# A diffusion block on one core: modulation vectors summed as 64 partial rows for each half of the columns

## Chip, cores and metric

The kernel runs on one core of a Trainium2 chip. The metric is the device time of one launch in microseconds; the time before is the median of three runs, 2196.51 us (2195.15 to 2198.44).

## The reference

Two blocks follow each other on a sequence of 256 tokens of width 1024, in fp32. The first has two layers of half an FFN (SwiGLU, 2816 wide), a token mixer with two attentions, and another half FFN. The second has two layers as well: retention and gated linear attention over a latent and a context stream, then windowed attention, each followed by an MLP of width 4096. Before and behind every part the stream is scaled, shifted and gated by modulation vectors of 1024 numbers:

```python
# first block, for each of 2 layers: 9 vectors
mod = jax.nn.silu(c) @ ada_w[l] + ada_b[l]          # ada_w[l]: 1024 x 9216
# second block, for each of 2 layers, once with c and once with c_ctx: 6 vectors
m = jax.nn.silu(cvec) @ w_mod[i] + b_mod[i]         # w_mod[i]: 1024 x 6144
```

So each vector is the product of one row of 1024 numbers with a 1024 x 1024 piece of weights, 4 MB. There are 38 of them that are used; the change touches 36, and the first two (`ada(0,1)` and `ada(0,0)`) are made in another way, which stays.

## The kernel before

All weights come from HBM. The large products run on PE in chunks of 1 MB of weights: 322 chunks, with three buffers. Each chunk is loaded by SP's queue into `stage`, ACT rounds it to the format of PE (`whi`, L1504, two halves of 128x1024), DVE takes the difference (`wlo`, L2027, two halves), and PE multiplies with both parts (L626 to L636, L733 to L735). PE waits for `lo_done` of a chunk; ACT waits for `chunk_used` before it overwrites a buffer. The order of work on every engine is written out by hand, chunk by chunk ("window" w below is what ACT and DVE do while PE works on chunk w of a phase). The phases are F0, in0, gate0, out0, F1, F2, in1, gate1, out1, F3, evc, evoc, evx, evox, Mc, M0, odc, odx, odo, M1; F are FFNs, in/gate/out a mixer, ev the retention part for context (c) and latent (x), M the MLPs, od the windowed attention.

Beside this stream the modulation vectors are made. A vector's weights are viewed as 8 blocks of 128 rows: row `k*128 + p` lies on partition p. POOL's queue loads them in four quarters of 1 MB (two k-blocks of 1024 columns, 4 KB runs) into one of two buffers `modw` (L607), each after both steps on the quarter two before are done. DVE makes eight steps for a vector (`mod_steps`, L2049 the first, a plain product; L2052 the seven others, product and sum), each over 128x1024 with a per-partition scalar `cact[:, which, t]`, the Silu of c, and each after the one before (semaphore `mod_step`). The result is 128 partial rows of 1024 columns. PE then transposes it in eight pieces of 128x128 into two banks of PSUM (`turn_mod`, L838), and DVE sums each transposed piece along its 128 columns (`take_mod`, L2060) into 8 columns of `mcol` and adds the bias (L2062). How many steps DVE makes in which window is a table:

```python
STEPS = {
    "F0": [0] + 22 * [1] + 4 * [2] + [0, 0, 1, 1, 0, 0],
    "in0": [2, 2, 2, 2, 0, 1, 1, 3, 3],
    "gate0": [2, 1, 1, 1, 1, 1, 1],
    "evc": [2, 2, 2, 0, 1, 1, 1, 2, 2, 1, 2, 0],
    "evx": [1, 1, 0, 1, 1, 0, 1, 2, 2, 2, 1, 0],
    "Mc": [0] + 3 * [1, 1, 1, 1, 2] + [1, 2, 0, 2, 2, 0, 1, 1, 0, 2, 2, 0, 1, 2, 0, 0],
    "M1": [0, 0] + 8 * [1] + 22 * [0],
}
```

F1 to F3 are as F0, in1 and gate1 as in0 and gate0, M0 as Mc. A turn stands on PE behind the window in which a vector's last step falls, or, in four cases, between the column sums of a normalisation and the filler products that keep PE busy until it is done (`rms_stat`).

At the start ACT's queue loads a part of the constants, the three vectors c as 24 rows of 128 (`crow`), and x; PE transposes `crow` (L900, its first instruction), ACT takes the Silu (`cact`). POOL meanwhile loads the eight quarters of the first two vectors, SP the biases and other small parameters. PE then sums the first two vectors (L922, L929) with filler products between, and SP's second weight chunks wait for their end (`rows1`).

## Time and profile before

| | |
|---|---|
| median of the runs | 2196.51 us |
| the profiled execution | 2197.7 us, its span 2195.9 us |
| PE busy | 2124.2 us, 97% |
| DVE busy | 1783.9 us, 81% |
| ACT busy | 1175.7 us, 54% |
| POOL busy | 109.5 us, 5% |
| mean share of the DMA engines | 69% |
| granted clock of PE, mean | 0.992 |

The span runs from the first to the last instruction. PE's busy time counts matmuls that overlap in the pipeline, so it says that PE had work, not that it was at its peak. What another engine adds counts only where PE, or whatever is last, waits for it; the chain of waits shows where.

### The profile page before, as it was taken

To read this page: it belongs to the slowest core of one execution; us is meant where nothing else is said; L and a number is where in the kernel's file an instruction comes from. 1 tells how busy PE (TensorE), PEld (TensorE's weight loads), DVE (VectorE), ACT (ScalarE), POOL (GpSimd) and SP (SyncE) were. 2 spreads that over 40 slices of the span, in tenths; PEclk is the share of its full clock that TensorE was granted. 3 is DMA by queue.
4 is the path that set the end of the run, shared out by engine and by line. 5 is a ranking of instruction groups with operands and counts; after the bars stand their busy time and mean duration, and the time that the engine had idled before them with its cause. 6 is when DMAs were issued, how large, how long until landed. Compare 5 with 4: busy or idle time off the path is not lost.

```text
span 2195.9 us, 33377 instructions
## 1 busy us (share of the span) xinstructions
PE 2124.2 (97%) x13779; PEld 1860.3 (85%) x13788; DVE 1783.9 (81%) x2366; ACT 1175.7 (54%) x1756; POOL 109.5 (5%) x157
## 2 busy tenths in 40 slices
PE   7999999999999999999999999999999999999997
PEld 4888888888888889898888889888888888768886
DVE  4888787788878878877888777788998998788764
ACT  3554556455455545665544645447645744485742
POOL 1000000000000000000000000000000000000000
PEclk9999999999999999999999999999999999999999
DMA  9888676488868877655887737638878977404662
GB/s 333 284 275 315 222 234 201 146 268 277 304 202 275 289 263 246 214 174 191 277 287 252 262 119 234 230 111 292 287 269 282 296 258 247 135 17 156 213 211 77
DMA packets 331023, 506.51 MB, mean 231 GB/s; under 512 B 12391, under 2 KB 239942, under 8 KB 330871
## 3 DMA queue, kind: packets, MB, share of 16 engines
q1 hardware_dynamic: 288647, 342.01, 47.4%
q0 software_dynamic: 41616, 160.44, 21.2%
q8 instruction: 109, 1.79, 0.3%
q10 hardware_dynamic: 608, 1.92, 0.3%
q14 instruction: 43, 0.35, 0.0%
HBM read 503.29 MB, written 1.05 MB: 230 GB/s over the span
## 4 chain that ended last, share of the span: by engine, by line
PE 83%; DVE 11%; DMA 3%; ACT 2%; issue 1%; POOL 0%; DVEq 0%; POOLq 0%
PE banks L632 36%; PE banks L636 18%; PE banks L626 6%; PE banks L628 6%; PE banks L627 6%; DVE wlo L2027 2%; DMA plain_xs<-in_ada_w_dram 1%; DVE arena L2052 1%; PE banks L838 1%; PE banks L733 1%; PE banks L900 1%; PE banks L734 1%; PE banks L735 1%; DMA modw<-in_w_mod_dram 1%; DMA stage<-in_ffn_wg_dram 1%
## 5 line engine op out<-in xcount | busy, mean ns | idle before, releaser
L2027 DVE TENSOR_TENSOR wlo<-stage,whi 128x1024 fp32r<-128x1024 f32 x644 | 758.3, 1219 | 133.6 <-ACT whi L1504 132.7
L1504 ACT CAST whi<-stage 128x1024 fp32r<-128x1024 f32 x644 | 643.9, 1051 | 336.2 <-PE banks L636 256.5
L632 PE MATMUL banks<-xs,whi 128*128 128x512 f32 x2176 | 688.2, 398 | 14.2 <-DVE xs L2309 9.6
L636 PEld LDWEIGHTS banks<-xs,wlo 128*128 128x128 f32 x2176 | 409.9, 188 | 97.0
L636 PE MATMUL banks<-xs,wlo 128*128 128x256 f32 x2176 | 428.6, 278 | 0.0
L626 PE MATMUL banks<-xs,whi 128*128 128x256 f32 x1216 | 352.0, 289 | 10.4 <-DVE xs L2309 5.7
L632 PEld LDWEIGHTS banks<-xs,whi 128*128 128x128 f32 x2176 | 332.3, 189 | 19.2 <-DVE xs L2309 7.6
L627 PE MATMUL banks<-xs,whi 128*128 128x256 f32 x1216 | 344.6, 283 | 0.0
L628 PE MATMUL banks<-xs,wlo 128*128 128x256 f32 x1216 | 344.5, 283 | 0.0
L632 PE MATMUL banks<-hidden_arena,whi 128*128 128x512 f32 x992 | 311.9, 396 | 0.2 <-DVE wlo L2027 0.2
L2052 DVE SCALAR_TENSOR_TENSOR arena<-modw,cact,arena 128x1024 f32<-128x1024 f32 x217 | 277.9, 1281 | 10.2 <-DMA modw<-in_w_mod_dram 7.2
L626 PEld LDWEIGHTS banks<-xs,whi 128*128 128x128 f32 x1216 | 233.6, 192 | 20.8 <-issue 9.1
L627 PEld LDWEIGHTS banks<-xs,whi 128*128 128x128 f32 x1216 | 233.8, 192 | 0.9 <-issue 0.5
L628 PEld LDWEIGHTS banks<-xs,wlo 128*128 128x128 f32 x1216 | 233.7, 192 | 0.0
L636 PEld LDWEIGHTS banks<-hidden_arena,wlo 128*128 128x128 f32 x992 | 186.5, 188 | 42.6
L636 PE MATMUL banks<-hidden_arena,wlo 128*128 128x256 f32 x992 | 195.8, 279 | 0.0
L632 PEld LDWEIGHTS banks<-hidden_arena,whi 128*128 128x128 f32 x992 | 150.1, 188 | 0.8 <-DVE wlo L2027 0.4
L607 POOL DMA_DIRECT2D modw<-in_w_mod_dram x80 | 57.1, 714 | 1139.7 <-DVE arena L2052 946.6
L632 PE MATMUL banks<-hs,whi 128*128 128x512 f32 x336 | 105.6, 395 | 0.0
L1524 ACT COPY hid<-banks 128x512 f32<-128x512 f32 x44 | 25.9, 588 | 112.8 <-PE banks L636 112.8
L607 POOL DMA_DIRECT2D modw<-in_ada_w_dram x64 | 45.7, 714 | 754.1 <-DVE arena L2052 669.1
L1520 ACT COPY hid<-banks 128x512 f32<-128x512 f32 x44 | 25.9, 588 | 106.0 <-PE banks L636 106.0
(438 smaller groups left out, 2628.8 us busy)
## 6 DMA issues: line engine op xcount, KB each, us to landing
stage<-in_mlp_w_dram SPq DMA_DIRECT2D x96, 1024.0 KB, 5.3
modw<-in_w_mod_dram POOLq DMA_DIRECT2D x80, 1024.0 KB, 5.8
modw<-in_ada_w_dram POOLq DMA_DIRECT2D x66, 1024.0 KB, 5.5
stage<-in_ffn_wg_dram SPq DMA_DIRECT2D x44, 1024.0 KB, 5.4
stage<-in_ffn_wu_dram SPq DMA_DIRECT2D x44, 1024.0 KB, 7.3
stage<-in_ffn_wd_dram SPq DMA_DIRECT2D x44, 1024.0 KB, 7.3
stage<-in_ev_w_in_dram SPq DMA_DIRECT2D x24, 1024.0 KB, 6.1
stage<-in_w_in_dram SPq DMA_DIRECT2D x18, 1024.0 KB, 6.0
```

The costliest lines, as they stand in the source:

```text
L607: pool.dma_start(modw[:, c % 2, :].rearrange("p (a b) -> p a b", a=2), src).then_inc(mod_landed[c % 2], 16)
L626: mm(out, hi, xh, start=first_mm, stop=False, skip_group_check=True)
L627: mm(out, hi, xl, start=False, stop=False, skip_group_check=True)
L628: return mm(out, lo, xh, start=False, stop=last_mm, skip_group_check=True)
L632: return mm(out, whi[:, s, w:w + P], pair.rearrange("p a t -> p (a t)"), start=first_mm, stop=False, skip_group_check=True)
L636: return mm(out[:, 0:T], wlo[:, s, w:w + P], pair[:, 0, :], start=False, stop=last_mm, skip_group_check=True)
L733: mm(out, xh, hi, start=k == 0, stop=False, skip_group_check=True)
L1504: nc.scalar.copy(halves(whi[:, s, :], n, h, True), halves(stage[:, s, :], n, h)).then_inc(hi_done, 1)
L1520: done(nc.scalar.copy(hid[:, j % 2, :, :], R[:, 0:2, T:2 * T]), ("gate", name, j))
L1524: done(nc.scalar.copy(hid[:, 2, :, :], R[:, 2:4, T:2 * T]), ("up", name, j - 1))
L2027: last = v.tensor_tensor(halves(wlo[:, s, :], n, h, True), halves(stage[:, s, :], n, h), halves(whi[:, s, :], n, h, True).bitcast(F32), AL ...
L2052: v.scalar_tensor_tensor(out=acc, in0=w, scalar=cc, in1=acc, op0=ALU.mult, op1=ALU.add).then_inc(mod_step, 1)
```

## The change

The 1024 rows of a vector's weights are viewed as 16 blocks of 64 rows. The left 512 columns are summed on partitions 0 to 63, the right 512 on partitions 64 to 127: 64 partial rows for each half, side by side on the partitions. A step of DVE is over 128x512, and there are 16 for a vector, two where one was. A quarter is loaded by two transfers of 64 partitions, each of four blocks by 512 columns (2 KB runs), and its semaphore counts 32. The transposes are four for a vector, all in one bank; in each transposed piece the left 64 columns belong to the left half's partial rows, the right 64 to the right half's, and one reduction over 128x512 sums both into the 8 columns. For the scalars, c is also laid out in blocks of 64, twice (`half_crow`, 48 rows of 128): six small transfers more on ACT's queue before x, one transpose more, and the Silu over 72 columns in place of 24. The first two vectors keep the old layout of c.

```diff
-        crow = table[0:24, 0:P]
+        crow, half_crow = table[0:24, 0:P], table[0:48, P:2 * P]
+        cact = cond[:, 0:24].rearrange("p (a k) -> p a k", a=3)
+        half_cact = cond[:, 24:72].rearrange("p (a k) -> p a k", a=3)
...
-        macc_of = lambda m: ACC_ROOMS[acc_name(m)]
+        macc_of = lambda m: ACC_ROOMS[acc_name(m)][:, 0:512]
...
-                for q, src in enumerate(quarters(*mods[m][0:3])):
+                w, l, v = mods[m][0:3]
+                rows = w[l].rearrange("(k p) n -> p k n", p=64)
+                for q in range(4):
                     c = 4 * m + q
                     if c >= 2:
-                        pool.wait_ge(mod_step, 2 * (c - 1))
-                    pool.dma_start(modw[:, c % 2, :].rearrange("p (a b) -> p a b", a=2), src).then_inc(mod_landed[c % 2], 16)
+                        pool.wait_ge(mod_step, 4 * (c - 1))
+                    for h in range(2):
+                        a = v * 1024 + 512 * h
+                        pool.dma_start(modw[64 * h:64 * h + 64, c % 2, :].rearrange("p (a b) -> p a b", a=4), rows[:, 4 * q:4 * q + 4, a:a + 512]) \
+                            .then_inc(mod_landed[c % 2], 16)
...
-                pe.wait_ge(mod_step, 8 * (m + 1))
+                pe.wait_ge(mod_step, 16 * (m + 1))
                 if m > 0:
                     pe.wait_ge(mod_taken, m)
-                for k in range(KB):
-                    last = nc.tensor.transpose(banks[:, k // 4, (k % 4) * P:(k % 4 + 1) * P], macc_of(m)[:, k * P:(k + 1) * P], ident)
+                for k in range(4):
+                    last = nc.tensor.transpose(banks[:, 0, k * P:(k + 1) * P], macc_of(m)[:, k * P:(k + 1) * P], ident)
                 last.then_inc(mod_turned, 1)
...
-            pe.wait_ge(c_landed, 48)
-            transpose(R[:, 2, 0:3 * KB], crow, 24).then_inc(pe_out.sem, pe_out.next("c"))
+            pe.wait_ge(c_landed, 144)
+            transpose(R[:, 2, 0:24], crow, 24)
+            transpose(R[:, 2, 24:72], half_crow, 48).then_inc(pe_out.sem, pe_out.next("c"))
...
+            for a, src in enumerate((A["c"].rearrange("b (k p) -> (b k) p", p=64), A["c_2"].rearrange("b (k p) -> (b k) p", p=64),
+                                     A["c_ctx_2"].rearrange("(k p) -> k p", p=64))):
+                for h in range(2):
+                    act.dma_start(half_crow[16 * a:16 * a + 16, 64 * h:64 * h + 64], src).then_inc(c_landed, 16)
             act.dma_start(xrows,
                           A["x"].rearrange("b (a p) d -> p (b a) d", p=P)).then_inc(x_landed, 16)
...
-                for _ in range(count):
-                    m, t = stepped[0] // 8, stepped[0] % 8
-                    stepped[0] += 1
-                    c = 4 * m + t // 2
-                    if t % 2 == 0:
-                        dve.wait_ge(mod_landed[c % 2], 16 * (c // 2 + 1))
-                    w = modw[:, c % 2, (t % 2) * 1024:(t % 2) * 1024 + 1024]
-                    cc = cact[:, mods[m][3], t:t + 1]
+                for i in range(2 * stepped[0], 2 * (stepped[0] + count)):
+                    m, t = i // 16, i % 16
+                    c = 4 * m + t // 4
+                    if t % 4 == 0:
+                        dve.wait_ge(mod_landed[c % 2], 32 * (c // 2 + 1))
+                    w = modw[:, c % 2, (t % 4) * 512:(t % 4) * 512 + 512]
+                    cc = half_cact[:, mods[m][3], t:t + 1]
...
                     if t == 0:
...
                     else:
-                        dve.wait_ge(mod_step, 8 * m + t)
+                        dve.wait_ge(mod_step, 16 * m + t)
                         v.scalar_tensor_tensor(out=acc, in0=w, scalar=cc, in1=acc, op0=ALU.mult, op1=ALU.add).then_inc(mod_step, 1)
...
-                v.tensor_reduce(cols, banks.rearrange("p a (k n) -> p (a k) n", k=4), AX_X, ALU.add).then_inc(mod_taken, 1)
+                v.tensor_reduce(cols.rearrange("p (h k) -> p h k", h=2), banks[:, 0, :].rearrange("p (k h n) -> p h k n", k=4, h=2), AX_X, ALU.add) \
+                    .then_inc(mod_taken, 1)
```

## Rows read from the trace of the kernel before

**Rows 1.** The page, busy time by engine.

```profile
PE 2124.2 (97%) x13779; PEld 1860.3 (85%) x13788; DVE 1783.9 (81%) x2366; ACT 1175.7 (54%) x1756; POOL 109.5 (5%) x157
```

**Rows 2.** The chain of work that ended last, by line, shares of the span.

```profile
by line: PE banks L632 36.2%; PE banks L636 18.0%; PE banks L626 6.2%; PE banks L628 6.0%; PE banks L627 6.0%; DVE wlo L2027 1.9%; DMA plain_xs<-in_ada_w_dram 1.3%; DVE arena L2052 1.1%; PE banks L838 1.1%; issue 1.1%; PE banks L733 1.0%; P
```

**Rows 3.** Groups by line and shape: count, busy us, mean ns, idle time before.

```profile
L2052 DVE SCALAR_TENSOR_TENSOR arena<-modw,cact,arena 128x1024 f32<-128x1024 f32 x217 | 277.9, 1281 | 10.2 <-DMA modw<-in_w_mod_dram 7.2 <-DVE mcol L2062 0.3 <-DMA modw<-in_ada_w_dram 0.2
...
L607 POOL DMA_DIRECT2D modw<-in_w_mod_dram x80 | 57.1, 714 | 1139.7 <-DVE arena L2052 946.6 <-DVE plain_hs L2052 104.4 <-DVE table L2052 83.1
...
L2060 DVE TENSOR_REDUCE mcol<-banks 128x8 f32<-128x1024 f32 x36 | 43.9, 1220 | 7.6 <-PE banks L838 7.5
...
L2049 DVE TENSOR_SCALAR arena<-modw,cact 128x1024 f32<-128x1024 f32 x31 | 23.3, 752 | 4.2 <-PE banks L838 3.5
...
L2812 DVE TENSOR_SCALAR arena<-arena,ecol 128x512 f32<-128x512 f32 x32 | 14.1, 484 | 0.6
...
L2451 DVE TENSOR_REDUCE ecol<-banks 128x2 f32<-128x512 f32 x16 | 11.0, 688 | 4.7 <-PE banks L982 4.4
...
L2523 DVE SCALAR_TENSOR_TENSOR arena<-arena,ecol 128x512 f32<-128x512 f32 x4 | 2.8, 750 | 0.3
```

**Rows 4.** Timeline of DVE: start, us, instruction.

```profile
1565.12 2.60 DVE L2052 SCALAR_TENSOR_TENSOR arena<-modw,cact,arena 128x1024 f32<-128x1024 f32 x2
1567.64 2.35 DVE L2027 TENSOR_TENSOR wlo<-stage,whi 128x1024 fp32r<-128x1024 f32 x2
...
385.82 0.75 DVE L2523 SCALAR_TENSOR_TENSOR arena<-arena,ecol 128x512 f32<-128x512 f32 x1
386.60 1.35 DVE L2229 TENSOR_TENSOR xs<-arena,xs 128x512 fp32r<-128x512 f32 x2
```

**Rows 5.** The chain in order of time: start, us, what.

```profile
276.22 0.87 PE banks L838 x8
...
295.57 1.21 DVE arena L2052
...
316.15 1.28 DVE plain_hs L2052
...
1240.81 1.28 DVE arena L2052
...
1404.29 5.54 DMA modw<-in_w_mod_dram
...
1591.61 5.53 DMA modw<-in_w_mod_dram
...
1626.40 7.53 DMA modw<-in_w_mod_dram
...
1833.45 1.06 PE banks L838 x8
```

**Rows 6.** Timeline of DVE in M0; in brackets the idle time and its releaser.

```profile
1779.60 1.28 DVE L2052 SCALAR_TENSOR_TENSOR arena<-modw,cact,arena 128x1024 f32<-128x1024 f32 x1 [0.90 <-DMA modw<-in_w_mod_dram]
...
1816.33 1.28 DVE L2052 SCALAR_TENSOR_TENSOR arena<-modw,cact,arena 128x1024 f32<-128x1024 f32 x1 [2.00 <-DMA modw<-in_w_mod_dram]
```

**Rows 7.** Waits: who for whom, us in total, times, longest.

```profile
DVE hid L2149 <- ACT hid L1556: 40.0, 41, 2.3
...
PE banks L1195 <- DVE hid L2654: 5.4, 1, 5.4
```

**Rows 8.** Timeline of the start, ACT queue and PE.

```profile
2.12 0.38 ACTq L1637 DMA_DIRECT2D table<-in_c_ctx_dram  x1
...
8.05 0.27 PE L900 MATMUL banks<-base,table 24*128 24x24 f32 x1 [8.05 <-DMA table<-in_c_ctx_dram]
...
34.04 1.98 PE L922 MATMUL banks<-plain_xs,cact 128*128 128x512 f32 x4 [0.27 <-DMA plain_xs<-in_ada_w_dram]
```

**Rows 9.** DMA issues: engine queue, count, KB each, us from issue to landing.

```profile
arena<-in_od_sink_dram SPq DMA_DIRECT2D x1, 8.0 KB, 8.9
arena<-in_ev_ret_theta_dram SPq DMA_DIRECT2D x1, 4.0 KB, 9.9
```

More of the change, by code:

```diff
@@ L153, in program @@
         pcol = sb("pcol", [P, 512])
-        cact = sb("cact", [P, 3, KB])
+        cond = sb("cond", [P, 9 * KB])
         mcol = sb("mcol", [P, 38 * KB])
@@ L1640, in _ @@
             act.wait_ge(pe_out.sem, pe_out.at("c"))
-            done(f(cact[:].rearrange("p a k -> p (a k)"), R[:, 2, 0:3 * KB], ACT.Silu), "cact")
+            done(f(cond[:], R[:, 2, 0:9 * KB], ACT.Silu), "cact")
             nc.scalar.preload_act_table_set(LN_EXP)
@@ L2050, in mod_steps @@
                     else:
-                        dve.wait_ge(mod_step, 8 * m + t)
+                        dve.wait_ge(mod_step, 16 * m + t)
                         v.scalar_tensor_tensor(out=acc, in0=w, scalar=cc, in1=acc, op0=ALU.mult, op1=ALU.add).then_inc(mod_step, 1)
+                stepped[0] += count
             def take_mod(banks):
```

## Prediction

> **What bounds the kernel now.** I read the page first: PE is busy 97% of the 2195.9 us span and DVE 81% [rows 1]. The reader is to see that a transpose saved on PE can count nearly anywhere, while work added on DVE counts only where DVE happens to be late. The chain of waits says how much of each lies on the path [rows 2]: the transposes (L838) hold 1.1% of the span, some 24 us, and the accumulating steps into `arena` (L2052) also 1.1%. One turn of eight transposes takes 0.87 us there [rows 5], so about 27 of the 36 turns are on the path; the other nine stand where PE waits for DVE, ACT or a transfer right afterwards. Read in order of time, the chain leaves PE for DVE in five places, and there the steps themselves are on it [rows 5]: in both mixers from the first step at 295.57 to the one at 316.15 (the second mixer repeats it), once in `evc` (1240.81), behind a transfer in `evx` (1404.29), and at the end of Mc, around the two transfers of 1591 and 1626. M0 has the same program as Mc; there DVE waits for two transfers [rows 6] and PE's turn at 1833.45 [rows 5] comes after a short idleness that I lay to the last steps.
>
> **Removed on PE.** Four of eight transposes a turn: half of 0.87 us, 0.435 us [rows 5], on 27 turns: -11.7 us. On the nine others the time turns into a longer wait for what was late already.
>
> **Changed on DVE.** A step over 1024 columns becomes two over 512 on twice as many k-blocks, each waiting for the one before.
> - Two dependent steps start 1.32 us apart (2.60 us for two, less one of 1.28), and what follows them without a dependence starts 1.20 us after the last began (1567.64 less 1565.12 is 2.52 for both) [rows 4]. A 512-column operation of this kind with a per-partition scalar takes 750 ns [rows 3] and the next began 0.78 us after it [rows 4]; independent work should follow after about 0.67, as 1.20 follows on 1.28. So an old step costs 1.20 at the end of a run and 1.32 within it, the new pair 0.78 + 0.67 = 1.45 and 0.78 + 0.78 = 1.56: **+0.25 us a step**, 252 of them. A bound from below is nothing, if a second engine were late at the same place; from above 1.50 less 1.20, 0.30.
> - The first step of a vector was a plain product of 752 ns; now it is one of 484 ns [rows 3] and an accumulating step behind it: about 0.52 + 0.67 against 0.68, **+0.5 us**, 36 times.
> - The reduction goes from 1220 to 688 ns [rows 3], **-0.53 us**, 36 times.
> In all DVE gets 63 + 18 - 19 = 62 us more. Most is hidden: in the MLP's first halves DVE waits 40.0 us in 41 windows for ACT's copy of PE's result, 1 us a window [rows 7], and a window has one step or two. What cover is left is thin in windows with two: 0.5 of it goes.
>
> On the path, counted along the chain: seven steps and one first step in each mixer, 14 x 0.25 + 2 x 0.5 = 4.5 us; one step in `evc`, 0.25; two in `evx` (one lets the transfer start, one follows it), 0.5; at the end of Mc seven steps, one first step and one reduction, 1.75 + 0.5 - 0.53 = 1.7; in M0 from the last point where PE sets the pace to the turn at 1833.45 eight steps, a first step and a reduction, 2.0 + 0.5 - 0.53 = 2.0. Sum **+8.95 us**. PE waits for these at the transposes or the masks behind them, and everything after is later by as much.
>
> The Trainium skill (VectorE: DVE Perf Modes, the section on the TRN2 errata) gives a two-tensor fp32 operation (N + 151)/0.96 ns, a fixed part of 157 ns an instruction, and so speaks against cutting one in two. By it a step would cost 0.16 us more and the 32 steps on the path 5.1 us in place of the 8.0 that my rows give; the difference is the wait for the step before, which its formula leaves out.
>
> **The weight quarters.** POOL issues two transfers of 64 partitions for one of 128: 714 ns more for each of 144 quarters [rows 3]. POOL itself waits for DVE most of the time, so this counts only where the landing ends a wait: 5.54 us in `evx`, 5.53 and 7.53 at the end of Mc [rows 5] and the two waits in M0 [rows 6]. The bytes are the same, and the second half is issued 0.71 us behind the first while the first still moves; so landing may be later by nothing, or by the whole 0.71, or, if the halves do not overlap, by more. Two ends: 0 and 2 us (a good third of a 5.5 us landing). I take 0.3: **+1.5 us** for five. Runs of 2 KB in place of 4 KB can add to it under load.
>
> The Trainium skill (DMA: Bandwidth & Descriptors, rules for kernel authors) says of two transfers to disjoint partition halves that they serialize and one of 128 partitions is to be used. With the fixed 2 us of its anatomy section paid twice each of the five landings would be 2 us later and the sum 8.5 us higher. No row here shows a split transfer.
>
> **The start.** Six small transfers more are queued on ACT ahead of `x`, and PE's first instruction waits for all nine (and ACT's Silu for PE). Now PE waits for the third of them until 8.05, though that was issued at 2.12 and took 0.38 us to issue [rows 8]. From there PE works without a gap, as the same timeline shows, up to 34.04, where it waits 0.27 us for the last first-vector quarter [rows 8]. So PE's slack is 0.27 us, and what comes behind is serial: the row sums, the chunk load that waits for them, F0's first chunks. Lower bound for the delay: six issues of some 0.4 us, 2.4 us. Upper: SP's small transfers issued 0.4 us apart land 1.4 apart (8.9 and 9.9 us after their issue [rows 9]), so 6 x 1.4 = 8.4. Those have 128 rows, the new ones 16; I take 4.0, less 0.27: **+3.7 us**. `x` also comes later, but PE reaches it later by as much. One more transpose (0.1 us) is left out.
>
> **The sum.** -11.7 + 8.95 + 1.5 + 3.7 = +2.5 us. The profiled execution took 2197.7 us (span 2195.9 and 1.8 around it), so it would take 2200.2; it stands 1.2 above the median of the runs, 2196.51, and against that the forecast is 2199.0, **no change that can be told**: about 0.2%, 4.4 us, is what a measurement of this kernel can tell from no change.
>
> **Rivals.**
> - *Faster: DVE is not the last at the five places.* If PE's own work there is as long as DVE's and the chain ran over DVE by a hair, the 8.95 us vanish, and the nine turns off the path gain 3.9 more: 2199.0 - 8.95 - 3.9 gives 2186. For it: PE is busy 97% of the span [rows 1], and at the end of Mc it hardly waits for DVE. Against: in `evx` it waits 5.4 us for DVE's mask [rows 7], and in each mixer, by the chain, for the probabilities. It decides from 6.9 us on, little more than half of it. Chance 0.13.
> - *Slower: the nine small transfers.* If each takes 1.4 us in the queue, the start costs 8.1 in place of 3.7: 2203.4. For it: the third of them, issued at 2.12, kept PE until 8.05 [rows 8]. It decides above a start of 5.6 us. Chance 0.2.
> - *Slower: the halves serialize.* 2 us more at five waits, 8.5 over my sum: 2207.5. It decides above 0.7 us a wait. For it: there are two buffers only, and the windows with two steps use up a quarter each. Against: the bytes are unchanged. Chance 0.13.
> - *Slower: DVE's cover runs out* in more Mc and M0 windows than the last ones, where it has 1 us a window for up to 0.5 added, or at the turns right behind two-step windows: some 0.5 us at a dozen windows, 6 us, 2205. Chance 0.06.
> - My forecast: 0.48, own range 2195 to 2203.
>
> **Chances and range.** Faster by over 0.2% (below 2192.1): most of the first rival, 0.11. Slower by over 0.2% (above 2200.9): nearly all of the three rivals on that side (0.39), 0.35, and the uppermost part of my forecast's own range, 0.05: 0.40. The same: 0.49. The range is 2190 to 2208: it takes in the first rival where it holds at three or four of the five places, and each of the others alone; outside stay the first rival in full and two of the others together.
>
> **What would show it.** L838: 144 transposes, turns of 0.44 us on the chain. L2052 (as it is then numbered): 504 + 36 of 750 ns and 36 products of 484; DVE's busy time up by some 50 us, since the busy times overlap less than the starts. The chain should hold more DVE at the five places, and PE's idle time should grow by 2.2 us in each mixer, before the mask in `evx` by 1.2 (0.8 of delay and the turn's 0.4), and before the turn at 1833 by some 4 (2.6 of delay and the saved transposes before it). PE's first transpose should stand at about 12 in place of 8.05, and F0's first chunks as much later. The quarters' landing, measured from the first half's issue, should be 5.5 to 6.2 us. I am wrong if the start moves by less than 2.4 or more than 8, if DVE's steps overlap although dependent, or if landings pass 7 us at the five waits.

## The result, and the profile after

The changed kernel took **2305.94 us**, median of four runs (2299.75 to 2316.13), against 2195.83 for the kernel before on the same chips; the ratio is 1.0506, 95% interval 1.0485 to 1.0527. It is 5% slower, 110 us, where I had forecast 2199.0 and a range up to 2208: the forecast was wrong, and so was every rival's size. All ratios here leave out executions in a slower state of the chip; there was one such, at 2304.53 us, among the four of `e10_halves_rows`.

The page of the changed kernel, read against [rows 1 and 2]. First busy time by engine, then the DMA queues (q1 is SP's, with the stage's chunks; q0 is POOL's, with the modulation weights; the last number is the share of 16 engines' span), then the chain by engine:

```profile
PE 2142.5 (93%) x13636; PEld 1866.3 (81%) x13645; DVE 1833.8 (80%) x2654; ACT 1176.4 (51%) x1756; POOL 184.4 (8%) x301
...
q1 hardware_dynamic: 288647, 342.01, 50.0%
q0 software_dynamic: 43920, 160.45, 30.4%
...
PE 53%; DVE 20%; DMA 20%; ACT 3%; issue 2%; POOL 0%; ACTq 0%; DVEq 0%; SPq 0%
```

The same two queue lines of the page of before:

```profile
q1 hardware_dynamic: 288647, 342.01, 47.4%
q0 software_dynamic: 41616, 160.44, 21.2%
```

POOL's stream carries the same 160.45 MB, and the DMA engines are busy with it for 30.4% of 2301 us, 700 us, where they had been for 21.2% of 2196, 466 us. SP's queue too takes more of their time for the same 342.01 MB: 50.0% of 2301 us, 1151 us, where it was 47.4% of 2196, 1041 us. DMA is 20% of the chain; it was 3%. Issue to landing (queue, count, KB each, median us), after and then before:

```profile
stage<-in_mlp_w_dram SPq DMA_DIRECT2D x96, 1024.0 KB, 8.6
modw<-in_w_mod_dram POOLq DMA_DIRECT2D x160, 512.0 KB, 8.5
...
stage<-in_ffn_wd_dram SPq DMA_DIRECT2D x44, 1024.0 KB, 14.1
```

```profile
stage<-in_mlp_w_dram SPq DMA_DIRECT2D x96, 1024.0 KB, 5.3
modw<-in_w_mod_dram POOLq DMA_DIRECT2D x80, 1024.0 KB, 5.8
...
stage<-in_ffn_wd_dram SPq DMA_DIRECT2D x44, 1024.0 KB, 7.3
```

Half a quarter now lands 8.5 us after its issue, a whole one took 5.8. And SP's chunks, which the change does not touch, are later too: `mlp_w` 8.6 for 5.3, `ffn_wd` 14.1 for 7.3. The groups by line and shape, for [rows 3]:

```profile
L1512 ACT CAST whi<-stage 128x1024 fp32r<-128x1024 f32 x644 | 643.1, 1050 | 494.2 <-DMA stage<-in_ffn_wd_dram 159.2 <-PE banks L643 122.7 <-DMA stage<-in_mlp_w_dram 110.9
...
L2063 DVE SCALAR_TENSOR_TENSOR arena<-modw,cond,arena 128x512 f32<-128x512 f32 x465 | 348.9, 750 | 68.6 <-DMA modw<-in_w_mod_dram 34.3 <-DMA modw<-in_ada_w_dram 23.7
...
L639 PE MATMUL banks<-hidden_arena,whi 128*128 128x512 f32 x992 | 321.3, 406 | 15.5 <-DVE wlo L2039 15.5
...
L613 POOL DMA_DIRECT2D modw<-in_w_mod_dram x160 | 98.7, 621 | 1169.2 <-DVE arena L2063 955.8 <-DVE plain_hs L2063 101.7 <-DVE table L2063 81.3
...
L2072 DVE TENSOR_REDUCE mcol<-banks 128x8 f32<-128x512 f32 x36 | 24.6, 685 | 0.0
...
L845 PE MATMUL banks<-base,arena 128*128 128x128 f32 x124 | 19.9, 285 | 13.7 <-issue 7.5 <-DVE arena L2063 6.3
...
L2060 DVE TENSOR_SCALAR arena<-modw,cond 128x512 f32<-128x512 f32 x31 | 15.0, 485 | 23.4 <-DMA modw<-in_w_mod_dram 12.5 <-DMA modw<-in_ada_w_dram 7.9 <-PE banks L845 2.4
```

The sum's prices are there: 750 ns a step, 485 the first, 685 the reduction, four transposes a turn. What is new stands behind the bars. The same two groups before:

```profile
L1504 ACT CAST whi<-stage 128x1024 fp32r<-128x1024 f32 x644 | 643.9, 1051 | 336.2 <-PE banks L636 256.5 <-PE banks L628 48.2 <-DMA stage<-in_mlp_w_dram 10.2
...
L632 PE MATMUL banks<-hidden_arena,whi 128*128 128x512 f32 x992 | 311.9, 396 | 0.2 <-DVE wlo L2027 0.2
```

ACT's cast (L1512, before L1504) waits 159.2 us for `ffn_wd` chunks and 110.9 for `mlp_w`; before, the second was 10.2 and the first 3.8 in all. DVE's steps in this group wait 58 us for their own weights. The end of it is PE's wait for `wlo`, 15.5 us in this one group, 0.2 before. The chain in order of time shows one such place, in the second half of F1 (start, us, what):

```profile
591.25 12.84 DMA modw<-in_ada_w_dram
...
609.53 17.50 DMA stage<-in_ffn_wd_dram
```

A half of a quarter lands 12.8 us after its issue and DVE waits for it; DVE then makes its `wlo` of a chunk and so frees the chunk's buffer late, and the next chunk loaded into it holds the chain for 17.5 us. Waits also cost PE its clock. At the start of F0 PE waits 5.0 us, until 66.41, and the mean granted clock from 60 to 70 us is 0.69 of full speed, between its two levels of 1.2 and 2.4 GHz (us, busy us of PE, PEld, DVE, ACT, POOL, clock, DMA share, GB/s):

```profile
50.00:60.00 10.00, 10.00 (x60) 8.76 (x59) 3.84 (x5) 0.59 (x1) 0.00 (x0) 1.00 1.05 243
60.00:70.00 10.00, 4.98 (x19) 4.02 (x19) 7.56 (x12) 8.75 (x11) 1.18 (x2) 0.69 0.98 315
```

The kernel before has such a place as well, a wait of 4.6 us until 57.79, and its clock then falls too. In the window from 50 to 60 us, where the DMA engines are busy throughout in both kernels, they move 310 GB/s there and only 243 in the changed one:

```profile
50.00:60.00 10.00, 5.41 (x25) 4.54 (x24) 5.22 (x6) 5.41 (x6) 0.00 (x0) 0.83 0.94 310
60.00:70.00 10.00, 10.00 (x50) 8.61 (x49) 9.90 (x15) 6.87 (x10) 0.71 (x1) 0.83 0.89 291
```

### The profile page after: what moved, and what is told of

Its sections match the earlier page's. It is cut to its first block, busy times and chain, and to the rows that moved or that the text cites. A ratio compares the mean times of both kernels' runs of the same rounds, so it can differ in the third digit from the quotient of the medians.

```text
span 2301.4 us, 33529 instructions
## 1 busy us (share of the span) xinstructions
PE 2142.5 (93%) x13636; PEld 1866.3 (81%) x13645; DVE 1833.8 (80%) x2654; ACT 1176.4 (51%) x1756; POOL 184.4 (8%) x301
## 3 DMA queue, kind: packets, MB, share of 16 engines
q1 hardware_dynamic: 288647, 342.01, 50.0%
q0 software_dynamic: 43920, 160.45, 30.4%
## 4 chain that ended last, share of the span: by engine, by line
PE 53%; DVE 20%; DMA 20%; ACT 3%; issue 2%; POOL 0%; ACTq 0%; DVEq 0%; SPq 0%
PE banks L639 19%; PE banks L643 10%; DVE wlo L2039 6%; DMA modw<-in_w_mod_dram 5%; PE banks L633 5%; PE banks L634 5%; PE banks L635 5%; DMA stage<-in_ffn_wd_dram 5%; DVE arena L2063 4%; DMA stage<-in_mlp_w_dram 4%; DMA modw<-in_ada_w_dram 2%; DMA stage<-in_ffn_wu_dram 2%; ACT whi L1512 1%; PE banks L907 1%; PE banks L740 1%
## 5 line engine op out<-in xcount | busy, mean ns | idle before, releaser
L1512 ACT CAST whi<-stage 128x1024 fp32r<-128x1024 f32 x644 | 643.1, 1050 | 494.2 <-DMA stage<-in_ffn_wd_dram 159.2
L2063 DVE SCALAR_TENSOR_TENSOR arena<-modw,cond,arena 128x512 f32<-128x512 f32 x465 | 348.9, 750 | 68.6 <-DMA modw<-in_w_mod_dram 34.3
L639 PEld LDWEIGHTS banks<-xs,whi 128*128 128x128 f32 x2176 | 333.5, 190 | 35.5 <-DVE hid L2162 14.1
L639 PE MATMUL banks<-hidden_arena,whi 128*128 128x512 f32 x992 | 321.3, 406 | 15.5 <-DVE wlo L2039 15.5
L643 PEld LDWEIGHTS banks<-hidden_arena,wlo 128*128 128x128 f32 x992 | 191.5, 193 | 45.3
L643 PE MATMUL banks<-hidden_arena,wlo 128*128 128x256 f32 x992 | 201.0, 284 | 0.0
L613 POOL DMA_DIRECT2D modw<-in_w_mod_dram x160 | 98.7, 621 | 1169.2 <-DVE arena L2063 955.8
L639 PEld LDWEIGHTS banks<-hidden_arena,whi 128*128 128x128 f32 x992 | 157.1, 194 | 18.2 <-DVE wlo L2039 17.6
L613 POOL DMA_DIRECT2D modw<-in_ada_w_dram x128 | 78.9, 621 | 753.4 <-DVE arena L2063 593.8
L643 PEld LDWEIGHTS banks<-hs,wlo 128*128 128x128 f32 x336 | 64.5, 192 | 15.5
L1532 ACT COPY hid<-banks 128x512 f32<-128x512 f32 x44 | 25.7, 585 | 91.1 <-PE banks L643 91.1
## 6 DMA issues: line engine op xcount, KB each, us to landing
stage<-in_ffn_wu_dram SPq DMA_DIRECT2D x44, 1024.0 KB, 10.2
stage<-in_ffn_wd_dram SPq DMA_DIRECT2D x44, 1024.0 KB, 14.1
```

What stands on the lines that cost most here:

```text
L613: pool.dma_start(modw[64 * h:64 * h + 64, c % 2, :].rearrange("p (a b) -> p a b", a=4), rows[:, 4 * q:4 * q + 4, a:a + 512]) \
L639: return mm(out, whi[:, s, w:w + P], pair.rearrange("p a t -> p (a t)"), start=first_mm, stop=False, skip_group_check=True)
L643: return mm(out[:, 0:T], wlo[:, s, w:w + P], pair[:, 0, :], start=False, stop=last_mm, skip_group_check=True)
L1512: nc.scalar.copy(halves(whi[:, s, :], n, h, True), halves(stage[:, s, :], n, h)).then_inc(hi_done, 1)
L1532: done(nc.scalar.copy(hid[:, 2, :, :], R[:, 2:4, T:2 * T]), ("up", name, j - 1))
L2063: v.scalar_tensor_tensor(out=acc, in0=w, scalar=cc, in1=acc, op0=ALU.mult, op1=ALU.add).then_inc(mod_step, 1)
```

## Experiments

Twelve further kernels were timed. My theory after the trace: a transfer to partitions 0-63, or to 64-127, fills them at a lower rate than one over all 128, and holds the DMA engines for longer; since all queues share these engines, SP's chunks come late as well. The rivals: the 2 KB runs; two issues for a quarter; 64 partitions in a transfer whichever they are; DVE's added steps and the start.

### The transfers by themselves

This kernel and the next compute nothing of the reference, and each ran once.

```python
for k, phase in enumerate((whole, halves_short, short_runs, halves_long, two_whole, only(0), only(32), only(64), whole)):
    n = 0
    for i in range(8):
        for dst, s in phase(i):            # one 1 MB transfer, or two of 512 KB
            pool.dma_start(dst, s).then_inc(sems[k], 16)
            n += 16
    pool.wait_ge(sems[k], n)
# halves_short: buf[64*h:64*h+64, i, :], 2 KB runs; only(at): buf[at:at+64, ...], 4 KB runs
```

> The disputed transfer by itself: 8 MB of fp32 from DRAM into a [128, 2048] buffer on the GpSimd queue alone, nine ways one after the other, each phase ending before the next begins; nothing of the reference is computed. In the kernel before, a packet of 4096 bytes of this stream takes a DMA engine about 159 ns and in the changed one about 298. Theory 1 (the half of the partitions: a destination of partitions 0-63 or 64-127 can be written only at half the rate, whichever engine carries it): the phases with 0-63 and 64-127, short runs or long, take about twice the time of the whole-partition phase, and so do those that fill only 0-63 or only 64-127; one that fills 32-95 and one that fills every second partition take the time of the whole. Theory 2 (2 KB runs): the phase of whole 128 partitions in 2 KB runs is as slow as the changed one, halves in 4 KB runs are fast. Theory 3 (two issues for a quarter): two transfers over 128 partitions are slow as well. Theory 5 (64 partitions in a transfer, whichever they are): 32-95 and every second partition are as slow as 0-63.

POOL's timeline; each line is the issues of one phase, so its start less the one before it is a phase of 8 MB:

```profile
1.29 5.74 POOL L164 DMA_DIRECT2D buf<-in_w_mod_dram  x8 [0.84 <-PEq L124]
25.85 9.83 POOL L164 DMA_DIRECT2D buf<-in_w_mod_dram  x16 [18.82 <-DMA buf<-in_w_mod_dram]
66.85 5.96 POOL L164 DMA_DIRECT2D buf<-in_w_mod_dram  x8 [31.17 <-DMA buf<-in_w_mod_dram]
91.75 9.37 POOL L164 DMA_DIRECT2D buf<-in_w_mod_dram  x16 [18.94 <-DMA buf<-in_w_mod_dram]
132.16 8.40 POOL L164 DMA_DIRECT2D buf<-in_w_mod_dram  x16 [31.04 <-DMA buf<-in_w_mod_dram]
156.36 9.39 POOL L164 DMA_DIRECT2D buf<-in_w_mod_dram  x16 [15.80 <-DMA buf<-in_w_mod_dram]
199.83 9.20 POOL L164 DMA_DIRECT2D buf<-in_w_mod_dram  x16 [34.08 <-DMA buf<-in_w_mod_dram]
224.49 9.35 POOL L164 DMA_DIRECT2D buf<-in_w_mod_dram  x16 [15.46 <-DMA buf<-in_w_mod_dram]
268.31 5.60 POOL L164 DMA_DIRECT2D buf<-in_w_mod_dram  x8 [34.47 <-DMA buf<-in_w_mod_dram]
292.71 1.11 POOL L168 DMA_DIRECT2D out_dram<-buf  x2 [18.80 <-DMA buf<-in_w_mod_dram]
```

Whole 24.6 us; halves in 2 KB runs **41.0**; whole in 2 KB runs 24.9; halves in 4 KB runs **40.4**; two whole transfers 24.2; 0-63 alone **43.5**; 32-95 alone 24.7; 64-127 alone **43.8**; whole again 24.4. Run length and number of issues are nothing here, and 64 partitions are as good as 128 if they are 32-95. (In the DMA packets of the trace the run length does not show: in runs of 2 KB and of 4 KB alike a phase has 2048 of 4096 bytes, beside 128 or 256 small ones.) Halves by turns run at 0.6 of the rate, one half alone at 0.56; theory 1 had said half of it. It is theory 1 in kind, and no rival.

Then the streams beside each other:

```python
phases = (second(i, 0), second(i, 1) on POOL       # buf[h::2, i, :], 2 KB runs
          half(i, 0) on POOL, half(i, 1) on ACT    # 0-63 and 64-127 from two queues
          chunk(i) on SP                           # 1 MB in 1 KB runs, as the stage
          whole(i) on POOL, chunk(i) on SP
          half(i, 0), half(i, 1) on POOL, chunk(i) on SP)
```

> Transfers by themselves again, 8 MB a stream, five phases, each ending before the next begins; nothing of the reference is computed. The first set of streams took 24.6 us for 8 MB over all partitions and 40 to 44 us for every form that goes to 0-63 and 64-127, while 32-95 alone took 24.7. Phase 1, two transfers of 64 partitions each, on every second partition: 25 us if it is which partitions that counts (theory 1), 40 us if it is their number. Phase 2, 0-63 from GpSimd's queue and 64-127 from ScalarE's at once: nearer 25 us if the two halves can be filled side by side, 40 us if not. Phase 3, SyncE's queue alone with the stage's pattern of 1 KB runs, 8 MB: some 25 us. Phase 4, that with the whole-partition stream beside it: 50 us for both. Phase 5, that with the stream in two halves: theory 1 says that the stage's stream suffers as well, the two together 60 us or more; if only the GpSimd stream were slowed, the two would fit beside each other in 50.

```profile
1.28 10.04 POOL L160 DMA_DIRECT2D buf<-in_w_mod_dram  x16 [0.84 <-PEq L124]
...
26.34 4.90 POOL L160 DMA_DIRECT2D buf<-in_w_mod_dram  x8 [15.02 <-DMA buf<-in_w_mod_dram]
60.26 133.14 SPq L160 DMA_DIRECT2D stage<-in_mlp_w_dram  x24
88.48 5.60 POOL L160 DMA_DIRECT2D buf<-in_w_mod_dram  x8 [57.24 <-DMA stage<-in_mlp_w_dram]
137.08 9.79 POOL L160 DMA_DIRECT2D buf<-in_w_mod_dram  x16 [43.00 <-DMA stage<-in_mlp_w_dram]
202.94 1.11 POOL L172 DMA_DIRECT2D out_dram<-buf  x2 [56.07 <-DMA stage<-in_mlp_w_dram]
```

(SP's line covers its issues of all three last phases; the third phase begins at 60.26 and ends at 88.48.) Every second partition: 25.1 us, full rate, with two transfers of 64. Halves from two queues at once: 33.9, between the 25 and the 40 that I had expected as the two possible outcomes. The stage's pattern alone: 28.2. With whole quarters beside it: 48.6; with halves: **65.9**. The two streams share one capacity: 28.2 and 24.6 make 52.8 in a row, 28.2 and 41.0 make 69.2, and together they take 3 to 4 us less than the sum. Each queue's share over the last phase, which ended with a chunk of the stage:

```profile
q0 software_dynamic: 2304, 8.39, 54.2%
q1 hardware_dynamic: 8320, 8.39, 47.7%
...
buf<-in_w_mod_dram POOLq DMA_DIRECT2D x16, 512.0 KB, 26.6
stage<-in_mlp_w_dram SPq DMA_DIRECT2D x7, 1024.0 KB, 24.1
```

The port rule of the Trainium skill (SBUF — State Buffer, section on door 1, the DMA port swizzle) says this beforehand: four consecutive partitions share a port, +32 is the same port again and +64 the other one of a pair, so 0-63 reaches 8 of 16 ports, and 32-95 and every second partition all of them. The runs agree with it at each of the five sets of partitions tried (43.5 and 43.8 us for the two 8-port ones, 24.4 to 25.1 us for the others); they show which partitions, not ports. The rule of the Trainium skill that my prediction cited (DMA: Bandwidth & Descriptors, rules for kernel authors), that two transfers to disjoint halves of the partitions serialize, gives no price, and the runs agree with it only in part: from one queue the halves take 41.0 us, nearly the 43.5 and 43.8 of one half alone, from two queues 33.9, and on even and odd partitions, which are disjoint halves too, 25.1.

### In the kernel before

```diff
-  pool.dma_start(modw[:, c % 2, :]..., src).then_inc(mod_landed[c % 2], 16)
+  for h in range(2):
+      pool.dma_start(modw[64 * h:64 * h + 64, c % 2, :]..., src[64 * h:64 * h + 64]).then_inc(mod_landed[c % 2], 16)
```

> The kernel before, computing the same; the only change: each quarter of the modulation weights is loaded by two transfers, one to partitions 0-63 and one to 64-127, in the same 4 KB runs as before. Steps, reductions, transposes and the start stay as before. Theory 1 (half of the partitions, at half the rate, with the stage loads slowed on the shared DMA engines): nearly the whole loss comes back, 2280 to 2310 us, and the landings of the stage loads rise (mlp_w from 5.3 to over 8 us). Theory 2 (2 KB runs) and theory 4 (DVE's added steps and the start): within 0.2% of before, about 2196. Theory 3 (two issues for a quarter): slow as well, here and in the two others of this set.

2277.91 us, ratio 1.0364 (1.0345 to 1.0383): 80 of the 110 us by this edit alone, just under the low end expected. (Here and below the count that DVE waits for changes with the number of transfers; the cuts of the edits leave this out.) Its queue and its issues:

```profile
q0 software_dynamic: 43920, 160.45, 30.4%
...
stage<-in_mlp_w_dram SPq DMA_DIRECT2D x96, 1024.0 KB, 8.2
modw<-in_w_mod_dram POOLq DMA_DIRECT2D x160, 512.0 KB, 8.6
```

The other two divide the same quarter without dividing the partitions, `modw[:, c % 2, 1024 * h:1024 * h + 1024]` from `src[:, h, :]`, and 512 columns of both k-blocks:

> The kernel before, computing the same; each quarter of the modulation weights is loaded by two transfers over all 128 partitions, one for each of its two k-blocks, in 4 KB runs. It has the second issue on GpSimd's queue (some 0.7 us more for each quarter) and nothing else of the change. Theory 1 (half of the partitions): 2196 to 2200 us. Theory 3 (two issues and two sets of descriptors for a quarter): some 5% slower, as the change.

2195.69 us, 0.9998 (0.9988 to 1.0007).

> The kernel before, computing the same; each quarter is loaded by two transfers over all 128 partitions, one for each half of the columns, so in runs of 2 KB in place of 4 KB, and with two issues. Theory 1 (half of the partitions): 2196 to 2205 us. Theory 2 (2 KB runs): most of the 110 us come back, 2280 us and more. Theory 3 (two issues): as slow as the run with two whole transfers of 4 KB runs.

2196.27 us, 0.9996 (0.9987 to 1.0006). Both rivals fall, and POOL's second issue costs nothing that can be told.

A dose: three transfers, `for lo, hi in ((32, 96), (0, 32), (96, 128))`.

> The kernel before, computing the same; each quarter by three transfers in 4 KB runs: partitions 32-95 (half of its bytes), 0-31 and 96-127 (a quarter each). The streams by themselves showed 32-95 filled at the full rate and 0-63 and 64-127 at some 0.57 of it. If the rate hangs on which partitions a transfer fills, 32-95 is free of the loss and the two outer ones bear it or part of it: the share of the DMA engines' time that the stream takes lies half way (26% of the span, between 21 and 30), and the time between 2196 and the 2278 of the two halves, about 2225 us. If 64 partitions or fewer in a transfer as such were slow, this is at least as slow as the two halves, 2278 us or more.

2230.13 us, 1.0142 (1.0117 to 1.0166), and:

```profile
q0 software_dynamic: 46224, 160.46, 26.4%
```

26.4% where 26 was expected, and five us above the time expected: there are more and smaller transfers, and the loss is less than half of that with two halves.

The changed kernel's own transfers in the kernel before, 2 KB runs and its rows (the edit is the change's loop over `rows`):

> The kernel before with the changed kernel's transfers and nothing else of it: 0-63 and 64-127, 2 KB runs, one half of the columns each. DVE's steps stay whole, so they multiply other weights than they should and the modulation vectors are of wrong values; the work is the same. The halves in 4 KB runs took 2278 us. Theory 1 alone, where the run's length does not count: 2275 to 2285 us. If the 30 us that are missing to the changed kernel are the short runs on top of the halves: 2300 us and more. If they are DVE's steps meeting later quarters: this stays at 2280 and the changed kernel with whole loads decides whether they cost anything by themselves.

2296.00 us, 1.0454 (1.0440 to 1.0468): above the 2285 of theory 1 alone, and just short of the 2300 for the short runs as all of the rest.

> The kernel before with each quarter in two halves, 0-63 and 64-127, in 4 KB runs, but with the changed kernel's rows (each half is two blocks of 64 whole rows). The steps then multiply other weights than they should, so the modulation vectors are of wrong values; the work is the same. The halves with before's rows in 4 KB runs took 2278 us, those with the changed kernel's rows and 2 KB runs 2296. If the length of the runs makes these 18 us, this takes 2278 us; if it is which rows go to a half (the order in which DRAM is read), 2296 us.

2282.42 us for all four, 1.0371 (1.0335 to 1.0407) for the three that the ratio counts, which lie between 2268 and 2284. The interval leaves out that of the 2 KB runs, so the 18 us are rather the short runs on top of the halves than the rows. Why runs of 2 KB cost something here and nothing in the stream by itself (41.0 against 40.4 us) is not settled.

### The change without its halves

```diff
-  for h in range(2):
-      a = v * 1024 + 512 * h
-      pool.dma_start(modw[64 * h:64 * h + 64, c % 2, :]..., rows[:, 4 * q:4 * q + 4, a:a + 512])...
+  pool.dma_start(modw[:, c % 2, :]..., w[l].rearrange("(k p) n -> p k n", p=P)[:, 2 * q:2 * q + 2, v * 1024:(v + 1) * 1024])...
```

> The changed kernel with one thing undone: each quarter is loaded by one transfer over all 128 partitions, as before; the split steps, four transposes, reductions and the start stay. The steps then multiply other weights than they should, so the modulation vectors are of wrong values; the work is the same. This is the prediction's sum without the weight quarters' term. Theory 1: 2197 to 2202 us, no change that can be told, or some of DVE's terms under-sized: 2205. Theory 4 (DVE's added steps and the start carry the rest of the loss, about 30 us, as the halves alone cost 80 of 110): 2225 us.

**2195.70 us**, 0.9998 (0.9989 to 1.0007), 1 us under the low end expected. All 110 us hang on how the quarters are loaded; the version on every second partition below, which keeps the two transfers and the 2 KB runs, narrows this to the partitions. Busy time by engine:

```profile
PE 2111.3 (96%) x13636; PEld 1845.4 (84%) x13645; DVE 1832.8 (84%) x2654; ACT 1175.2 (54%) x1756; POOL 109.5 (5%) x157
```

PE executes the same 13636 matmuls as in the changed kernel, in 31.2 us less busy time (mean granted clock 0.992 against 0.978) and with 82.6 us of idle span against 158.9. So of the 107.5 us between the two spans 76 are waits and 31 longer PE time for the same matmuls. I lay the 31 to the clock, which falls after waits as in the window at 60 us; no run separates the two. In the window from 50 to 60 us, with the same late start, this kernel moved 370 GB/s where the changed one had moved 243.

The start of a turn's first weight load says where my sum's parts went (us; differences to before, one profiled execution of each kernel. That of before is late by some 1.5 us from the start on, if the two kernels with divided whole quarters are the measure, 1.8 and 1.4 ahead at turn 0; "mixed" is the last version below):

| turn (place) | before | changed, whole loads | mixed |
|---|---|---|---|
| 0 | 99.4 | -3.8 | -4.1 |
| 4, before mixer 0 | 276.0 | -5.3 | -5.5 |
| 5, behind it | 388.1 | -2.5 | -5.1 |
| 15, before mixer 1 | 854.5 | -5.5 | -7.6 |
| 16, behind it | 966.7 | -3.4 | -5.5 |
| 21 and 22, evc | 1187.2, 1258.3 | -5.0, -4.1 | -6.6, -6.9 |
| 24 and 26, evx | 1406.0, 1505.5 | -4.5, -3.2 | -6.9, -7.3 |
| 28 and 29, end of Mc | 1579.7, 1626.2 | -4.0, -3.1 | -7.6, -8.1 |
| 33 and 34, M0 | 1792.5, 1833.4 | -4.7, -1.9 | -8.7, -7.8 |

### The start alone

The kernel before with the six small transfers, the second transpose and the Silu over 72 columns, nothing else:

> The kernel before with nothing of the change but the start: the six small transfers of c in half rows on ScalarE's queue ahead of x, one transpose more, and Silu over all 72 columns. It computes the reference. The prediction priced this part at +3.7 us (2199.7 from the 2196.0 of before). The traces of the changed kernel with whole loads, with every second partition and of before say otherwise: PE's first product of F0 comes 2.2 us later there than before, but a wait of 4.6 us that the kernel before has at 57.8 is 1.1 us there at 62.0, and at the first turn both are 4 us ahead. If that is the later start itself (what the stage's second chunk waits for no longer makes PE wait, and the granted clock stays at 1.00 there), this kernel takes 2193 to 2195 us and its first turn is about 3 us earlier than before's. If it comes from the split steps instead, this kernel is 2 to 4 us slower than before.

2196.02 us, 0.9996 (0.9988 to 1.0005): neither the 3.7 us more of the prediction nor the 1 to 3 us less that I expected here. Its first turn is 2.8 us ahead of before's profiled execution, some 1.2 ahead of the two kernels that share the old start. PE's longest weight wait at the start of F0, here and before, and before also ACT's cast of the late chunk (start, us, instruction, idle time before it):

```profile
63.09 0.73 PE L633 MATMUL banks<-xs,whi 128*128 128x512 f32 x2 [1.33 <-DVE hid L2093]
```

```profile
57.79 1.22 PE L632 MATMUL banks<-xs,whi 128*128 128x512 f32 x2 [4.59 <-DVE hid L2083]
...
53.70 1.99 ACT L1504 CAST whi<-stage 128x1024 fp32r<-128x1024 f32 x2 [9.76 <-DMA stage<-in_ffn_wg_dram]
```

These are waits for different chunks. Before, PE waits for the second gate chunk (`ffn_wg`), issued at 37.77 and cast only at 53.70. With the late start this chunk is issued at 41.00, but ACT casts it already at 46.83 and PE passes its place without a wait; PE waits one chunk later, for the up chunk (`ffn_wu`), cast at 57.90 where it was at 57.05. So both chunks together are there at nearly the same time with either start (the DMA engines' share was 0.94 from 50 to 60 us before), and with the late start in the better order. Why the order changes was not tried.

### A version with every second partition, and a mixed one

Besides what is shown, `c` is laid out to match, by three small transfers and one copy on DVE in place of six small transfers.

```diff
-  pool.dma_start(modw[64 * h:64 * h + 64, c % 2, :]..., rows[:, 4 * q:4 * q + 4, a:a + 512])
+  pool.dma_start(modw[h::2, c % 2, :]..., rows[:, 4 * q:4 * q + 4, a:a + 512])
-  banks[:, 0, :].rearrange("p (k h n) -> p h k n", k=4, h=2)
+  banks[:, 0, :].rearrange("p (k n h) -> p h k n", k=4, h=2)
```

> The changed kernel with the two halves of the columns laid on the even and the odd partitions in place of 0-63 and 64-127; still two transfers of 64 partitions for a quarter, in 2 KB runs. c is laid out to match, by three small transfers and one copy on DVE in place of six small transfers, and the reduction reads the banks in another order. It computes the reference. Theory 1 (which partitions): as the changed kernel with whole loads, 2197 to 2203 us. Theory 5 (64 partitions in a transfer as such): about 2300 us, as the change.

**2194.70 us**, 0.9992 (0.9983 to 1.0001), 2 us under the low end expected and not to be told from before. The same two transfers of 64 partitions and 2 KB runs as in the change, and:

```profile
q0 software_dynamic: 43920, 160.45, 20.9%
...
stage<-in_mlp_w_dram SPq DMA_DIRECT2D x96, 1024.0 KB, 5.5
modw<-in_w_mod_dram POOLq DMA_DIRECT2D x160, 512.0 KB, 5.0
```

20.9% of the span for the stream, less than before's 21.2; a half lands in 5.0 us.

```diff
+  WHOLE = (5, 16, 22, 25, 26, 29, 34)   # these vectors as before: 8 steps, whole quarters, 8 transposes
```

> The changed kernel with its halves on every second partition, and seven of the 36 vectors (numbers 5, 16, 22, 25, 26, 29 and 34, those whose steps the chain of waits runs through: one in each mixer, one in evc, two around evx, one at the end of Mc, one in M0) done as before the change: whole steps, one transfer of 128 partitions for a quarter, eight transposes. It computes the reference. In the changed kernel with whole loads, the turns off these places move the rest ahead by 0.3 to 0.5 us each, 8.8 us in all, and at the seven it loses 10.8 us again. If those are the steps on the path, this kernel keeps the 8.8 and the 2 of the start and loses hardly anything: 2184 to 2188 us, faster by 0.4%. If PE's gain only turns into another wait (a stage load, ScalarE), it takes 2193 to 2196 us as the version on every second partition did.

**2190.64 us** (2189.12 to 2191.07), ratio 0.9969 (0.9956 to 0.9981): 0.3% faster than the kernel before, small but outside its interval, and 3 us short of what I had expected. Steps in mixer 0, evc, evx and Mc cost at most 0.5 us now and in M0 0.9; mixer 1 still loses 2.1 us (table). There the granted clock is 0.83 for a stretch, where it was 1.00 before:

```profile
890.00:900.00 10.00, 8.29 (x52) 6.34 (x51) 9.76 (x19) 6.75 (x20) 0.50 (x1) 0.83 0.65 211
```

and PE waits 1.7 us for ACT's probabilities in each mixer, where it was 0.9 before; in the changed kernel with whole loads it was 1.7 as well. Why ACT is later there, with whole steps too, was not tried.

## Why the prediction was wrong

**The step that failed** is the term for the weight quarters: "The bytes are the same, and the second half is issued 0.71 us behind the first while the first still moves; so landing may be later by nothing, or by the whole 0.71, or, if the halves do not overlap, by more." I took +0.3 us at five waits, 1.5 us; the runs put the whole loss there. It failed twice. *In the rate*: I took equal bytes for equal DMA time. A half takes 0.6 of the rate, so 1 MB costs 5.1 us of the engines in place of 3.1 (41.0 and 24.6 us for eight). *In who pays*: I counted the five landings that already ended a wait, as if the rest were hidden and as if the stream met nobody. The DMA engines were 69% busy before, 47.4% with SP's queue and 21.2% with POOL's. POOL's stream took 234 us more of them and SP's own 110 more, which made 81%, and SP's 322 chunks, which carry PE's work, came late. The average hides how full they are where it counts: from 440 to 700 us their share was 0.81 before and 0.90 after. The halves landed 8.5 us after their issue, past the 7 us that I had named as a sign of being wrong. My rival "the halves serialize" had the sign and a mechanism nearby, and priced it at 2 us for each of five waits, 8.5 us in place of 110.

Without this term my sum gives 2197.5, and the changed kernel with whole loads measured 2195.7. That this is near is partly luck: the transposes gained 2.9 us less than said and DVE's steps cost 1.8 more; against these 4.7 us stand the 3.7 us of the start, which did not come, and some 2 us that this run had gained by its first turn.

- *Transposes*, -11.7 us: four a turn as said. In the table's run the turns off the five places and M0 move it ahead by 0.2 to 0.5 us each, four of them by nothing, 8.8 in all (summed over the single turns from turn 0 on; the table has only some). At most the size of a turn was as said; their number on the path was too high, some 20 by the 0.435 us for 27.
- *DVE's steps*, +8.95 us: DVE's busy time rose by 48.9 us (some 50 predicted). At the five places and M0 that run loses 10.7 us again, net of the turns there: 2.8 and 2.1 in the mixers (2.25 each predicted), 0.9 in evc (0.25), 1.3 in evx (0.5), 0.9 at the end of Mc (1.7), 2.7 in M0 (2.0). The wait for evx's mask is 6.5 us for 5.4, +1.1 (1.2 predicted). The places were right; evc, evx and M0 were under-sized and the end of Mc over-sized. The faster rival, that DVE is not the last there, falls, and so does the one that its cover runs out elsewhere. One reading beside the sum was off: the prediction lays all of the 0.09 us between its step price and the one by the formula of the Trainium skill (VectorE: DVE Perf Modes, the section on the TRN2 errata) to the wait for the step before. From its own rows two steps of 750 ns less one of 1281 are 0.22 us without any wait, so the wait is only 0.03 of it.
- *The start*, +3.7 us: wrong, by more than its bounds, and the rival that the nine small transfers cost still more falls with it. PE's first transpose stands at 10.84 in the changed kernel (8.05 before, 12 predicted), and its first product of F0 came 2.6 us later, so the delay itself was within the bounds. But behind it PE was held up by F0's second chunks in any case, and these were there at 57 to 58 us with the early start and the late one: 4.6 us of waiting and a lower clock before, 1.3 us with the late start alone, which measures as nothing. I had followed the serial chain to F0's first chunks and stopped before the next wait; a delay is only priced when the wait behind it has been read.

What stays open: halves in 4 KB runs explain 80 us, the change's own transfers 100, the changed kernel 110. The last 10 are what the edits leave to DVE's split steps, the turns and the start on top of late quarters, though together these cost nothing without them; that they delay the issue of the next, slower quarter is argued from the chain at 591 us, not shown. Nor is the size of the loss worked out: 344 us more of the DMA engines' time became 110 us of the kernel's, and no sum here leads from the one to the other.

## What to carry to other kernels

Choose the partitions of a transfer as carefully as its bytes: a buffer cut at partition 64 was filled at 0.6 of the rate, the same halves laid on every second partition at the full one, and the sums need only another order of reading. Price a slower transfer by the DMA engines' time first, before asking which landings end a wait; equal bytes say nothing. The queue's share of the span times the ratio of the rates gives an estimate, here 466 us times 1.67 or 777 us, where 700 were measured. Compare it with what the other queues leave free stage by stage: on the average 31% was free here, and the loss came all the same. And follow a delay at the start up to the next wait that was there already, since it may be no later with the delay than without.

## What the runs showed of the hardware that was not expected

- 8 MB into 128 partitions took 24.6 us, into 0-63 and 64-127 by turns 41.0, into 0-63 alone 43.5, into 32-95 alone 24.7, into every second partition by turns 25.1; in runs of 2 KB or 4 KB alike.
- Halves 0-63 and 64-127 from two queues at once took 33.9 us for 8 MB: they overlap in part.
- A slow transfer takes its time from the other queues: the stage's 8 MB beside halves finished 17 us later than beside whole quarters (65.9 against 48.6). In the kernel SP's queue took 1151 us of the DMA engines for the bytes that had taken 1041.
- POOL's issue of a 512 KB transfer took 621 ns in the changed kernel, where one of 1 MB took 714: two cost 528 ns more than one, not 714. It went with the form of the transfer: 529 ns for one run of 4 KB on each of 128 partitions, 592 for two of 4 KB on 64, 621 for four of 2 KB on 64, 723 for two of 2 KB on 128.
